# Stationary operands of an expert layer: high and low parts interleaved element by element, 256 bytes past a multiple of 512

## The reference

```python
logits = (xt @ router).astype(F32)
top_v, top_i = lax.top_k(logits, TOP_K)          # 2 of 8
gates = jax.nn.softmax(top_v, axis=-1)
combine = jnp.sum(jax.nn.one_hot(top_i, N_EXPERTS, dtype=F32) * gates[..., None], axis=1)
for e in range(N_EXPERTS):
    out = out + combine[:, e:e + 1] * (silu(xt @ w1[e]) * (xt @ w3[e])) @ w2[e]
```

## Time and profile before

| | us |
|---|---|
| median of 3 runs (lowest, highest) | 1505.19 (1504.82, 1506.57) |
| the profiled execution, its own time | 1508.43 |
| its span, first to last instruction | 1506.6 |
| TensorE matmul busy | 1479.1 (98%) |
| TensorE weight load busy | 1297.6 (86%) |
| VectorE busy | 1236.9 (82%) |
| ScalarE busy | 962.0 (64%) |
| expert layer, from the first row of L2495 to the last of L2544 | 544.6 to 1493 |

### The profile page before, as it was taken

One profiled execution on the slowest core, in us unless ns is written; L12 is line 12 of the kernel. 1 busy time (PEld: TensorE's weight loads), 2 busy tenths in 40 slices (PEclk: granted clock), 3 DMA queues, 4 the chain that ended last, 5 costly groups with the idle time before them and its releaser, 6 DMA issues.

```text
span 1506.6 us, 23455 instructions
## 1 busy us (share of the span) xinstructions
PE 1479.1 (98%) x8803; PEld 1297.6 (86%) x8804; DVE 1236.9 (82%) x906; ACT 962.0 (64%) x693; POOL 83.8 (6%) x65
## 2 busy tenths in 40 slices
PE   9998999999999999999999999999999999999997
PEld 8987899999999978888888888888888888888885
DVE  6898866656578779889888888888888888988987
ACT  6644353333353567777777777777777777777774
POOL 1035200000000030000000000000000000000300
PEclk9999999999999999999999999999999999999998
DMA  8745697888654669999999999999999999999990
GB/s 311 225 131 157 221 342 267 305 297 300 228 182 168 228 227 413 403 367 389 376 381 382 373 393 375 377 385 376 382 392 359 387 395 361 388 385 364 407 413 36
DMA packets 212938, 483.97 MB, mean 321 GB/s; under 512 B 8810, under 2 KB 26314, under 8 KB 209820
## 3 DMA queue, kind: packets, MB, share of 16 engines
q1 hardware_dynamic: 209224, 473.67, 85.2%
q10 hardware_dynamic: 2388, 5.32, 1.0%
q0 software_dynamic: 1280, 4.33, 0.7%
HBM read 446.45 MB, written 36.87 MB: 321 GB/s over the span
## 4 chain that ended last, share of the span: by engine, by line
PE 86%; DVE 1%; issue 0%; ACT 0%; DVEq 0%
PE Q L2544 20%; PE Q L2495 14%; PE Q L2497 14%; PE Q L2496 14%; PE Q L2039 7%; PE Q L2040 7%; PE Q L2041 7%; PE Q L2528 2%; DVE wlo L1174 1%; PE Q L2474 0%; PE Q L2505 0%; ACT yrows L1149 0%; PE Q L2400 0%; PE Q L2408 0%; PE Q L2032 0%
## 5 line engine op out<-in xcount | busy, mean ns | idle before, releaser
L1174 DVE TENSOR_TENSOR wlo<-raw,whi 128x2048 fp32r<-128x2048 f32 x413 | 940.3, 2297 | 186.2 <-ACT whi L988 109.3
L988 ACT ACTIVATE whi<-raw 128x2048 fp32r<-128x2048 f32 x336 | 642.2, 1919 | 169.8 <-PE Q L2497 81.1
L2495 PE MATMUL Q<-whi,xgh 128*128 128x512 f32 x896 | 354.2, 395 | 0.0
L2497 PE MATMUL Q<-whi,xgl 128*128 128x512 f32 x896 | 349.6, 390 | 0.0
L2496 PE MATMUL Q<-wlo,xgh 128*128 128x512 f32 x896 | 348.9, 389 | 0.0
L2039 PE MATMUL Q<-xh,whi 128*128 128x264 f32 x1024 | 294.7, 288 | 5.4 <-DVEq L1285 1.8
L2040 PE MATMUL Q<-xl,whi 128*128 128x264 f32 x1024 | 292.0, 285 | 0.0
L2041 PE MATMUL Q<-xh,wlo 128*128 128x264 f32 x1024 | 290.7, 284 | 0.0
L2039 PEld LDWEIGHTS Q<-xh,whi 128*128 128x128 f32 x1024 | 193.8, 189 | 8.1 <-issue 4.1
L2497 PEld LDWEIGHTS Q<-whi,xgl 128*128 128x128 f32 x896 | 168.1, 188 | 35.8
L2496 PEld LDWEIGHTS Q<-wlo,xgh 128*128 128x128 f32 x896 | 168.5, 188 | 33.6
(11 more groups left out here) (286 smaller groups left out, 1138.8 us busy)
## 6 DMA issues: line engine op xcount, KB each, us to landing
raw<-in_moe_w SPq DMA_DIRECT2D x336, 1024.0 KB, 7.1
raw<-in_ffn_w SPq DMA_DIRECT2D x42, 1024.0 KB, 7.3
raw<-in_hgrn_w_in SPq DMA_DIRECT2D x16, 1024.0 KB, 7.3
xg_rows<-zeros SPq DMA_DIRECT2D x6, 2048.0 KB, 10.9
y_rows<-zeros SPq DMA_DIRECT2D x6, 2048.0 KB, 11.7
raw<-in_conv_w_in SPq DMA_DIRECT2D x12, 1024.0 KB, 5.4
raw<-in_hgrn_w_out SPq DMA_DIRECT2D x4, 1024.0 KB, 5.0
raw<-in_conv_w_out SPq DMA_DIRECT2D x4, 1024.0 KB, 5.1
```

Of the source, the lines that this page charges most:

```text
L988: a.activation(bufs(q)[0], raw[:, n % RAW, PW * (q % 2):PW * (q % 2 + 1)], ACT.Copy).then_inc(hi_done, 1)
L1174: v.tensor_tensor(low, raw[:, slot, PW * half:PW * (half + 1)], high.bitcast(F32), ALU.subtract).then_inc(lo_done, 1)
L2495: t_.matmul(out, xgh[:, kt, :], high[:, w], start=(kt == 0), stop=False)
L2497: mm = t_.matmul(out, xgl[:, kt, :], high[:, w], start=False, stop=(kt == DT - 1))
```

## The change

The two parts of a stationary tile share one tensor with a last axis of 2: `xgp` holds `xgh` and `xgl`, `htp` holds `hth` and `htl`, and `htp_last` the two last ones. The old names become views of every second element. So the 128 elements of a tile now lie 8 bytes apart over 1024 bytes. `xs` stays where it is, and all that follows is moved up by `LIFT` = 256 bytes, so that the stationary tiles begin 256 bytes past a multiple of 512 (low parts 4 bytes later). `whi`, `wlo`, `whi2` and `wlo2` keep their addresses. No instruction is added, removed or moved: each engine issues the same instructions in the same order, and only the operands' addresses and steps differ. Those touched are the weight loads of L2495 to L2497 and L2544, the writes of L1049, L1056, L1087 (ScalarE), and the writes and one input of L1786, L1794, L1894 (VectorE). `xg`, `hs`, `hx`, `pick`, `yl` and the small tensors of the routing are contiguous as before, 256 bytes further up.

```diff
+        LIFT = 256
...
-        (xs, xgh, xgl, xg, hs, hx, hth, htl), o = region(
-            R0, ("xs", [P, TT, D], F32), ("xgh", [P, DT, P], F32R), ("xgl", [P, DT, P], F32R),
+        (xs,), o = region(R0, ("xs", [P, TT, D], F32))
+        (xgp, xg, hs, hx, htp), o = region(
+            o + LIFT, ("xgp", [P, DT, P, 2], F32R),
             ("xg", [P, D], F32), ("hs", [P, FW], F32), ("hx", [P, FW], F32),
-            ("hth", [P, 4, P], F32R), ("htl", [P, 4, P], F32R))
+            ("htp", [P, 4, P, 2], F32R))
+        xgh, xgl, hth, htl = xgp[:, :, :, 0], xgp[:, :, :, 1], htp[:, :, :, 0], htp[:, :, :, 1]
...
-        (hth_last,), _ = region(xgh_at, ("hth_last", [P, 4, P], F32R))
-        (htl_last,), _ = region(xgh_at + size([P, DT, P], F32R), ("htl_last", [P, 4, P], F32R))
+        (htp_last,), _ = region(xgh_at, ("htp_last", [P, 4, P, 2], F32R))
+        hth_last, htl_last = htp_last[:, :, :, 0], htp_last[:, :, :, 1]
```

## The result

The changed kernel takes 1529.96 us (median of 5 runs, 1529.81 to 1533.58) against 1505.19 us: a ratio of 1.0168, 95% interval 1.0154 to 1.0182. It is slower by 24.8 us, far outside the range of the forecast.

What follows compares the result with a forecast made beforehand. TensorE's distance from matmul to matmul, mostly in the expert layer, was taken as the bound. All terms summed to 0, so the forecast stayed at the median, 1505.2 us, range 1502 to 1508 (over the cases 1457 to 1512).

Steps and rivals of the forecast that it cites:

- What bounds the kernel: TensorE holds 86% of the span; each of 4032 expert-layer matmuls takes 226.7 ns, 13.3 ns above its columns.
- The weight load itself: 4032 expert-layer loads reading 8 bytes apart: 0 us, with up to 38 ns more per load covered by the matmul beside it.
- The bound of 107 ns: Upper bound on extra time per expert-layer weight load, if the rate of reading elements halves.
- What the load does to the moving stream: Load's effect on the 13.3 ns surplus per expert-layer matmul: taken as 0, ends minus 44.4 and plus 53.8 us.
- After a turn: Longer distances after the four transposes, 0.10 us, 56 times: change taken as 0, between minus 5.6 and plus 5.6 us.
- The copies: ScalarE's `hth` (592 ns) and VectorE's `htl` (684 ns) writing at 8 bytes: stay as they are, cost 0.
- Moved up 256 bytes: Everything shifted by 256 bytes is read and written as before: 0; the 12 `pick` matmuls bounded at 0.16 us.
- That the surplus is a collision of places: Faster rival, expert-layer matmuls: new layout avoids load-stream collisions; 1461 us in full (0.20), partly or only after turns 0.18.
- two walks at equal pace that never meet: Faster rival's picture: stepped load and moving stream both walk 9.6 bytes per ns, starting 256 bytes apart.
- That the load touches twice the memory: Slower rival at the 4032 expert-layer distances: twice the span doubles the surplus to 240 ns per matmul, 1559 us; chance 0.08.
- A stretch after turns twice as bad: Weaker slower rival: the long distances after the transposes get twice as bad, 1511 us; chance 0.10.
- The load as the bound: Slower rival: at half rate a load takes 295 ns, outlasting its matmul; 286 us more, 1791 us; chance 0.04.

Runs made afterwards that it cites:

- e4: Kernel before, with only `hth` and `htl` (down projection) at 16 bytes from element to element, beginning at a multiple of 512: 1519.73 us, ratio 1.0092.
- e5: Kernel before, contiguous tiles, but each expert-layer load takes 8 columns in place of 128: 1502.58 us beside 1504.98.
- e6: Kernel before, with tiles interleaved (step 8 bytes) at multiples of 512 and each expert-layer load taking 8 columns: 1538.26 us beside 1504.98.
- e1: Kernel before, stationary tiles still contiguous but beginning 256 bytes past a multiple of 512: 1505.55 us, ratio 0.9999.
- e2: Kernel before, with stationary tiles interleaved (step 8 bytes), beginning at a multiple of 512: 1530.93 us, ratio 1.0167.
- e9: Kernel before, contiguous tiles; `xgh` begins 64 bytes and `hth` 32 bytes past a multiple of 512: 1532.2 us beside 1505.07.
- e15: Kernel before, contiguous stationary tiles plus moving `whi2` and `wlo2` all 64 bytes past a multiple of 512, `whi` and `wlo` left: 1520.93 us beside 1510.35.
- e10: Kernel before, stationary tiles unchanged, moving tiles `whi2` moved by 32 and `wlo2` by 64 bytes: 1518.81 us beside 1505.07.
- e14: Kernel before, contiguous tiles; `xgh` begins 96 bytes and `hth` 160 bytes past a multiple of 512: 1534.18 us beside 1510.35.
- e8: Kernel before, with tiles interleaved (step 8 bytes) at multiples of 512 and expert-layer loads of 64 columns in place of 128: 1515.17 us beside 1504.98.
- e16: Kernel before, with moving-tile rows of layer 0's down projection padded from 1056 to 1280 bytes: 1505.55 us, ratio 0.9996.

## Why the prediction was wrong

**What bounds the kernel.** Right: the whole of the 25 us lies in TensorE's distances, at a granted clock of 1.00, and nobody else became late. One reading is off without consequence: not 53 rows but 47 of 54 take 5.44 us; the seven that come after the transposes of the gathered rows take 5.48 or 5.49.

**The weight load itself**, taken as 0: right. The record grew by 7 ns and stayed inside the 38 ns of cover. The bound of 107 ns would have needed a step of 16 bytes (311 ns, e4), and even then the distance rose by 8.5 ns only. The cover is also larger than I said: a load of 311 ns goes beside matmuls 235 ns apart, so a load's record is not all time that it keeps TensorE from the next.

**What the load does to the moving stream**, taken as 0 with ends of minus 44.4 and plus 53.8 us: this step failed. It was plus 6.96 ns per matmul, 28 us, about half of the upper end. The argument rested on the earlier trace rows: with 8 columns the distance is the same 226.7 ns. The row was read correctly, and e5 repeats it 4032 times. What does not follow from it is that the load has no part. I had only asked whether the surplus is paid per column loaded. The price is not paid per column, nor per byte; it goes by where the load reads against where the stream reads, and e6 pays 8.6 ns more with the same 8 columns. `pick` and `yh` lie 256 bytes apart, which I took as a second placement without effect; by e1 that is a shift that changes nothing. Both tests of the earlier trace rows stood at the same good place.

**After a turn**, taken as 0 within 5.6 us. Before, the first distance after the transposes is 316 ns, the next nine lie between 224 and 236, and then they hold 226.67. With the change the distances go at once into the pattern that they keep. The nine distances after each set of transposes, 576 in the layer, take 132.98 us before and 134.53 with the change, 1.5 us more where 6.96 ns each would be 4.0. These 2.5 us are most of the difference between 28.1 and the 25.2 us measured. With 8 columns (e5) the settling is over after one matmul, and the layer takes 945.9 us, 2.2 less: of the 5.6 us less than half was settling, the rest is the step from the transposes to the first matmul.

**The copies**, 0: right in effect. ScalarE took 46 ns more, which I had not expected at a step of 8 bytes, and VectorE none; 4 us of cover held.

**Moved up 256 bytes**, 0: right (e1).

**The rivals.** That the surplus is a collision of places was the nearest in mechanism, and I gave it the wrong sign: the contiguous kernel was already where it collides least, and the new layout met more of it. My picture of two walks at equal pace that never meet is refuted, for the interleaved tiles at 0 and at 256 bytes go equally (e2). That the load touches twice the memory gave the right sign and place, at 13.3 ns where 7 were paid; as a mechanism it falls with e9, which touches no more and pays 6.7, and with e6, which touches little and pays most. A stretch after turns twice as bad, 1511 us, did not come; the change loses less there. The load as the bound did not come either, and my sum for it was off: 295 less 226.7 is 68 ns, not 71, which makes 1780 us and not 1791.

The Trainium skill's section Who interferes with whom in SBUF — State Buffer gives TensorE two independent read ports, from which I took that the load can't be the cause. The trace disagrees: e15 has two distances, 226.67 and 233.33 ns, that differ in the relative places of two reads, with the same place and a record of 187 to 188 ns for the load. Two ports of its own do not keep the load from having a part in TensorE's pace.

What stays open is the arrangement behind it: the distances are 544, 552 and 560 cycles of 2.4 GHz for 226.67, 230.0 and 233.33 ns, which looks like steps of 8 cycles, but why 32 bytes cost what 64 do and 192 less, no run tells. Nor does any run tell why the distance remembers what came before (e10). Places finer than 32 bytes were not tried, and whether the last 13.3 ns, which no place removed, have the same cause is not shown.

## What to carry to other kernels

Where TensorE is the bound and each matmul has its own weight load, the places of stationary and moving tiles relative to each other are a parameter: in fp32r with 512 columns and contiguous tiles they moved the distance from 226.7 to as much as 234.3 ns, and the layer by 2.7% (e14). For contiguous tiles, begin both at a multiple of 256 bytes, the best of what was tried here, and measure after each change of a layout, even one that moves no instruction. A test that shows no effect at one place shows none at that place only; before it is used to exclude a mechanism, ask which of its inputs it varied.

## What was not expected of the hardware

- A contiguous load of 188 ns at 32 or 64 bytes in place of 0 costs each matmul 6.7 ns (e9). With a step of 8 bytes at 0, one of 8 columns costs 8.6 to 8.9 ns, one of 64 columns 3.3 and one of 128 columns 6.9 (e6, e8, e2).
- At a good relation the distances lock: 226 or 227 ns after some ten matmuls (e1), and in the dense part 121.7, 116.7, 121.7 ns by turns (e16). At a bad one they stay near 233 ns (e15), or go up and down around that mean: 236 and 231 by turns (e9), in the change 238 and 229 by turns or 234, 235 and 238 in some experts.
- Writing 512 elements with a step of 8, 12 and 16 bytes takes ScalarE 638, 870 and 1098 ns against 592; VectorE, which reads one input with the same step, takes 684, 873 and 1109 against 684.
- A weight load takes 188, 195, 252 and 311 ns at steps of 4, 8, 12 and 16 bytes, and the matmuls' distance is 226.7, 233.6, 235.5 and 235.2.
